# Earlier gathers for the expert mixer: aligned row places, the first two heads picked singly, five gathers ahead of the last two weight splits

## What is computed

```
q = (xt @ w_query).reshape(t, PEER_HEADS, 2, PEER_KEY_DIM // 2)          # 8 heads, 2 x 64
s = jnp.einsum('thkd,hknd->thkn', q, sub_keys)                           # 2 x 128 sub-keys a head
vals, idx = lax.top_k(s, PEER_TOPK)                                      # 16 of each
cand = (vals[:, :, 0, :, None] + vals[:, :, 1, None, :]).reshape(...)    # 256 sums
best, pos = lax.top_k(cand, PEER_TOPK)                                   # 16 experts a head
...
expert = (i1 * N_SUB_KEYS + i2).reshape(t, PEER_HEADS * PEER_TOPK)       # 128 picks a token
gate = jax.nn.softmax(best, axis=-1)
a = jnp.einsum('cd,ced->ce', xb, u_tab[eb])
w = gb * jax.nn.gelu(a, approximate=False)
out = jnp.einsum('ce,ced->cd', w, v_tab[eb])
```

## Time and profile before

| | us |
|---|---|
| median of 3 runs | 4531.28 (4531.2 to 4533.3) |
| profiled execution, its own time | 4529.67 |
| its span | 4527.9 |
| PE busy | 4151.7 (92%) |
| DVE busy | 2505.7 (55%) |
| POOL busy | 1957.4 (43%) |
| ACT busy | 1320.4 (29%) |
| software DMA queue (the gathers) | 536.9 MB, 28.6% of the 16 engines' span |

### The profile page before, as it was taken

One profiled execution on the slowest core, in us unless ns is written; L12 is line 12 of the kernel. 1 busy time (PEld: TensorE's weight loads), 2 busy tenths in 40 slices (PEclk: granted clock), 3 DMA queues, 4 the chain that ended last, 5 costly groups with the idle time before them and its releaser, 6 DMA issues.

```text
span 4527.9 us, 49208 instructions
## 1 busy us (share of the span) xinstructions
PE 4151.7 (92%) x15840; PEld 2816.4 (62%) x15840; DVE 2505.7 (55%) x4408; ACT 1320.4 (29%) x2903; POOL 1957.4 (43%) x1612
## 2 busy tenths in 40 slices
PE   7999987787787787899999999999999999999998
PEld 4567753333333333388876676888888867767886
DVE  7967676766767675544235545543343264536442
ACT  2224222222222222332223332322232233333322
POOL 4333543333333333354454353444444544445443
PEclk8999999989999999899999999999999999999999
DMA  5112279999999999732322121223223212112232
GB/s 140 42 59 82 79 317 421 421 421 421 421 412 421 421 406 422 292 102 95 96 84 65 44 91 63 94 97 94 95 96 96 95 56 70 59 63 95 96 94 83
DMA packets 160595, 806.06 MB, mean 178 GB/s; under 512 B 17488, under 2 KB 25088, under 8 KB 94848
## 3 DMA queue, kind: packets, MB, share of 16 engines
q0 software_dynamic: 73728, 536.90, 28.6%
q1 hardware_dynamic: 81952, 260.15, 17.8%
q10 hardware_dynamic: 4704, 6.42, 0.8%
HBM read 798.17 MB, written 5.24 MB: 177 GB/s over the span
## 4 chain that ended last, share of the span: by engine, by line
issue 27%; PE 25%; POOL 19%; DMA 14%; DVE 11%; DVEq 1%; ACT 1%; POOLq 1%; ACTq 0%
POOL wl L621 10%; PE bank L1015 6%; DMA rows_o<-in_peer_uv,expert 6%; POOL wl L590 6%; PE bank L674 5%; PE bank L676 5%; PE bank L675 5%; DMA rows_x<-in_peer_uv,expert 4%; DMA rows_w<-in_peer_uv,expert 4%; POOL wh L588 2%; DVE rows_o L2091 1%; DVE rows_w L2091 1%; DVE hst L1869 1%; DVE rows_x L2091 1%; POOLq L589 1%
## 5 line engine op out<-in xcount | busy, mean ns | idle before, releaser
L621 POOL TENSOR_TENSOR wl<-raw,wh 128x1024 fp32r<-128x1024 f32 (+3 forms) x304 | 726.4, 2390 | 831.1 <-ACT wh L1510 831.1
L674 PE MATMUL bank<-xh,wh 128*128 128x512 f32 x2368 | 945.0, 399 | 1.6 <-DVE oraw L2256 1.6
L676 PE MATMUL bank<-xh,wl 128*128 128x512 f32 x2368 | 924.9, 391 | 0.0
L675 PE MATMUL bank<-xl,wh 128*128 128x512 f32 x2368 | 923.3, 390 | 0.0
L674 PEld LDWEIGHTS bank<-xh,wh 128*128 128x128 f32 x2368 | 445.5, 188 | 144.0 <-issue 51.3
L1510 ACT ACTIVATE wh<-raw 128x1024 fp32r<-128x1024 f32 x304 | 320.7, 1056 | 729.5 <-PE bank L676 584.3
L676 PEld LDWEIGHTS bank<-xh,wl 128*128 128x128 f32 x2368 | 445.2, 188 | 95.0
L675 PEld LDWEIGHTS bank<-xl,wh 128*128 128x128 f32 x2368 | 446.0, 188 | 89.1 <-issue 1.9
L590 POOL TENSOR_TENSOR wl<-raw,wh 128x1024 fp32r<-128x1024 f32 (+2 forms) x234 | 479.2, 2048 | 34.8 <-issue 1.9
L1015 PE MATMUL bank<-rows_o,diag 128*128 128x512 f32 x688 | 340.8, 653 | 90.3 <-ACT diag L1476 90.3
L1015 PE MATMUL bank<-rows_w,diag 128*128 128x512 f32 x672 | 329.0, 647 | 95.0 <-ACT diag L1476 95.0
(11 more groups left out here) (414 smaller groups left out, 6432.0 us busy)
## 6 DMA issues: line engine op xcount, KB each, us to landing
raw<-in_w_l SPq DMA_DIRECT2D x324, 512.0 KB, 3.2
raw<-in_w SPq DMA_DIRECT2D x58, 512.0 KB, 3.2
raw<-in_w_l SPq DMA_DIRECT2D x64, 448.0 KB, 3.3
raw<-in_w_l SPq DMA_DIRECT2D x48, 256.0 KB, 2.6
raw<-in_w SPq DMA_DIRECT2D x16, 256.0 KB, 2.6
bias_scratch<-brow ACTq DMA_DIRECT2D x1, 3072.0 KB, 33.5
raw<-in_uq_l SPq DMA_DIRECT2D x16, 192.0 KB, 2.3
rows_o<-in_peer_uv,expert POOLq DMA_INDIRECT x172, 18.1
```

Source lines behind the costliest of these rows:

```text
L621: gp.tensor_tensor(wl[:, slot, 0:w], raw[:, rslot, 0:w], f32(wh[:, slot, 0:w]), ALU.subtract).then_inc(w_split.sem, 1)
L674: pe.matmul(bank[b][:], wh[:, slot, c], ah, start=k == 0, stop=False)
L675: pe.matmul(bank[b][:], wh[:, slot, c], al, start=False, stop=False)
L676: mm = pe.matmul(bank[b][:], wl[:, slot, c], ah, start=False, stop=k == last)
```

## The change

Five things, in one edit:

- The first buffer, the area behind the constants and `rows_o` start on multiples of 512 bytes, so that every row place does. `work` moves to behind `wl`, three small buffers become one.
- Heads 0 and 1 are picked one after the other instead of together. `SUB_KEY_PARTS` has (0, 0, 1), (0, 1, 1) in place of (0, 0, 2); PE forms the scores of head 0 after half of query 1 and those of head 1 after half of query 2. `p_pick` and `p_best` count one more.
- Gathers 0 to 4 stand ahead of POOL's splits of query 6 and 7. In these two splits the low part waits for the high part by a semaphore, `high_written`, in place of the drain.
- There are 14 row places for the first round and 13 from then on: `work` is one more, and `raw` serves once, for gather 5. The order is `o0` to `o3`, `work`, (`raw`), `w1`, `w3`, `w0`, `w2`, `x0` to `x3`. `w1` and `w3` wait for query 5 to be done, `w0` and all behind it for query 7.
- SP's first load of the second block waits until row 5, the one in `raw`, has been mixed.

`pick_experts` also copies the positions in two instructions, where it was one, in every window.

```diff
-        base = (nc.sbuf_base + 63) // 64 * 64
+        base = (nc.sbuf_base + 511) // 512 * 512
...
-        region = (top[0] + 127) // 128 * 128
+        region = (top[0] + 511) // 512 * 512
...
+        a.o = (a.o + 511) // 512 * 512
         rows_o = a("rows_o", [P, 4, 2 * D])
...
+        RING_ROWS = ["o0", "o1", "o2", "o3", "work", "w1", "w3", "w0", "w2", "x0", "x1", "x2", "x3"]
+        FIRST_ROWS = RING_ROWS[:5] + ["raw"] + RING_ROWS[5:]
+        row_of = FIRST_ROWS + [RING_ROWS[n % len(RING_ROWS)] for n in range(NB * PICKS - len(FIRST_ROWS))]
...
+        RAW_FREE = 1 + row_of.index("raw")
...
-        SUB_KEY_PARTS = [(0, 0, 2), (0, 2, 2), (0, 4, 4)] + [(tc, h0, 4) for tc in range(1, NB) for h0 in (0, 4)]
+        SUB_KEY_PARTS = [(0, 0, 1), (0, 1, 1), (0, 2, 2), (0, 4, 4)] + [(tc, h0, 4) for tc in range(1, NB) for h0 in (0, 4)]
...
+            sp.wait_ge(p_mixed, RAW_FREE)
...
-                gp.tensor_copy(wh[:, slot, 0:w], raw[:, rslot, 0:w])
-                gp.drain()
+                high = gp.tensor_copy(wh[:, slot, 0:w], raw[:, rslot, 0:w])
+                if behind_fetch:
+
+                    high.then_inc(high_written, 1)
+                    gp.wait_ge(high_written, behind_fetch)
+                else:
+                    gp.drain()
...
+            def fetch(n):
+
+                if n == 0 or n == TOPK:
+                    gp.wait_ge(p_pick, n // TOPK + 1)
+                elif n % WINDOW == 0:
+                    gp.wait_ge(p_pick, n // WINDOW + 2)
+                if row_of[n] == "raw":
+
+                    gp.wait_ge(w_split.sem, w_split.at(TILES_1, None))
+                if row_last[n] is not None:
+                    gp.wait_ge(p_mixed, row_last[n] + 1)
+                elif row_of[n] in ("w1", "w3"):
+
+                    gp.wait_ge(product.sem, product.at(TILES_1 - 2, None))
+                elif row_of[n] == "w0":
+
+                    gp.wait_ge(product.sem, product.at(TILES_1, None))
...
+            for j in range(6):
+                split(AT_1["query"].tile0 + j, None, KD)
+
+            for n in range(5):
+                fetch(n)
+            for j in range(6, 8):
+                split(AT_1["query"].tile0 + j, None, KD, behind_fetch=j - 5)
+            for n in range(5, NB * PICKS):
+                fetch(n)
...
-            linear(query, 1, None, normed)
+            linear(query, 1, None, normed, share=(0, 2))
+            pe.wait_ge(*read_at(query, 0, None))
+            sub_key_scores(0)
+            linear(query, 1, None, normed, share=(1, 2))
             linear(query, 2, None, normed, share=(0, 2))
-            pe.wait_ge(*read_at(query, 0, None))
             pe.wait_ge(*read_at(query, 1, None))
-            sub_key_scores(0)
+            sub_key_scores(1)
...
-            for q in range(2):
-                pick_keys(q)
-                pick_pairs(q)
-                pick_experts(q)
+            for q, heads in ((0, (0,)), (0, (1,)), (1, both)):
+                pick_keys(q, heads)
+                pick_pairs(q, heads)
+                pick_experts(q, heads)
```

More of the change, by code:

```diff
@@ L43 @@
 RAWS = 2
-ROWS = 12
 WINDOW = 2 * TOPK
@@ L305, in build @@
         rows_w = at("rows_w", [P, 4, 2 * D], F32, base + 4 * KD * T * 3 + 4 * RAWS * KD * P)
-        rows = [t[:, b, :] for t in (rows_o, rows_x, rows_w) for b in range(4)]
-        ROWS_W_FREE = 1 + max(n for n in range(NB * PICKS) if n % ROWS >= 8)
+        flat_row = lambda t: t[:].rearrange("p a t -> p (a t)")
+        row_tiles = {**{f"{c}{b}": t[:, b, :] for c, t in (("o", rows_o), ("x", rows_x), ("w", rows_w)) for b in range(4)},
+                     "work": flat_row(work), "raw": flat_row(raw)}
+        RING_ROWS = ["o0", "o1", "o2", "o3", "work", "w1", "w3", "w0", "w2", "x0", "x1", "x2", "x3"]
+        FIRST_ROWS = RING_ROWS[:5] + ["raw"] + RING_ROWS[5:]
+        row_of = FIRST_ROWS + [RING_ROWS[n % len(RING_ROWS)] for n in range(NB * PICKS - len(FIRST_ROWS))]
+        row_use = [row_of[:n + 1].count(r) for n, r in enumerate(row_of)]
+        row_last = [max([m for m in range(n) if row_of[m] == r], default=None) for n, r in enumerate(row_of)]
+        RAW_FREE = 1 + row_of.index("raw")
+        ROWS_W_FREE = 1 + max(n for n, r in enumerate(row_of) if r[0] == "w" and r != "work")
         psum = ctx.enter_context(nc.psum_tensor("bank", [P, 8 * T], F32))
@@ L379, in build @@
         p_gate = sem("p_gate")
-        fetched = [sem(f"fetched{i}") for i in range(ROWS)]
+        high_written = sem("high_written")
+        fetched = {r: sem(f"fetched_{r}") for r in FIRST_ROWS}
         p_dot = sem("p_dot")
@@ L571, in _, with split @@
             gp.wait_ge(made, 3)
-            def split(n, l, nblk, extra=0, turns=0):
+            def split(n, l, nblk, extra=0, turns=0, behind_fetch=0):
                 glob = n if l is None else TILES_1 + n
@@ L2008, in top16, with pick_keys @@
                 settle()
-            def pick_keys(q):
-                n = q if q < 2 else q // 2 + 1
+            both = (0, 1)
+            def pick_keys(q, heads=both):
+                n = heads[0] if q == 0 else 2 if q == 1 else q // 2 + 2
                 if q < 2 or q % 2 == 0:
-                    tc, h0, heads = SUB_KEY_PARTS[n]
+                    tc, h0, n_heads = SUB_KEY_PARTS[n]
                     h0 %= 4
@@ L2031, in pick_pairs, with pick_experts @@
                 settle()
[L2032 removed]
+                top16([(cand[:, h, :, :].rearrange("p a b -> p (a b)"), h) for h in heads], 2 * SUBK,
                       lambda key, o: best[:, key, o:o + 8], lambda key, o: pos[:, key, o:o + 8])
[L2035 to L2040 removed]
+            def pick_experts(q, heads=both):
+                hs = slice(heads[0], heads[-1] + 1)
+                grid = [P, len(heads), TOPK, TOPK]
+                dve.tensor_scalar(posh[:, 0, hs, :], pos[:, hs], 4, None, ALU.logical_shift_right)
+                dve.tensor_scalar(posh[:, 1, hs, :], pos[:, hs], 15, None, ALU.bitwise_and)
@@ L2051, in pick_experts @@
-                e0, e1 = (eid[:, k, :, :].rearrange("p h k -> p (h k)") for k in range(2))
+                cols = slice(q * WINDOW + heads[0] * TOPK, q * WINDOW + (heads[-1] + 1) * TOPK)
+                e0, e1 = (eid[:, k, hs, :].rearrange("p h k -> p (h k)") for k in range(2))
                 dve.scalar_tensor_tensor(expert[:, cols], e0, float(SUBK), e1, ALU.mult, ALU.add).then_inc(p_pick, 1)
-                dve.tensor_tensor(pgate[:, cols].rearrange("p (h k) -> p h k", h=2), best[:],
-                                  best[:, :, 0:1].to_broadcast([P, 2, TOPK]), ALU.subtract).then_inc(p_best, 1)
+                dve.tensor_tensor(pgate[:, cols].rearrange("p (h k) -> p h k", h=len(heads)), best[:, hs],
+                                  best[:, hs, 0:1].to_broadcast([P, len(heads), TOPK]), ALU.subtract).then_inc(p_best, 1)
```

73 lines of the change are left out of this document (32 added, 41 removed).

## The result

| | before | changed |
|---|---|---|
| median, us | 4531.9 (4531.2 to 4533.3, 4 runs) | 4488.4 (4487.8 to 4489.2, 4 runs) |
| profiled execution, its own time | 4529.67 | 4488.83 |
| its span | 4527.9 | 4486.7 |
| last dot product | 1889.62 | 1868.32 |
| from there to the end | 2638.3 | 2618.4 |

The ratio is 0.9904, 95% interval 0.9892 to 0.9916. The last two lines of the table show where to look: 21.3 us are gained by the last dot product, and 19.9 behind it, in the two layers that the forecast let "move as a whole".

A forecast was written before the change was run, and what follows sets the result against it. The gather stage's full DMA queue was taken as the bound, 2.48 us a gather. Terms 9.9 - 0.3 - 2.5 = 7.1 us off 4529.67 gave 4522.6, plus 1.6 for the median 4524.2; range 4517 to 4533.

The forecast's parts named there:

- move as a whole: Behind the last gather: the same dots, drain and splits follow unchanged, so no gain or loss there.
- Aligned places: Gather stage: row places on multiples of 512 bytes change nothing, priced at 0.
- The rival at 4500: Gather stage: alignment shortens packets, 24 us if half the fixed packet cost came from misaligned places; chance 8%.
- Eight gathers ahead, 9.9 us: Start of gather stage: eight instead of four gathers through before the wait for query 7 ends, 9.9 us gained.
- The lead: Gather 14, waiting for row 0 to be mixed: queue stays fed, gap 0 to 0.8 us, taken as 0.
- head 1's pass: DVE's picking of head 1 after head 0: 10.7 us, 60% of the two-head pass.
- SP's loads, 2.5 us: Second block's first two loads wait for row 5, about 631, into a full queue: 2.5 us lost.
- PE's scores, 0.3: PE before query 7's end: scores in three pieces instead of two add 0 to 0.65 us, taken as 0.3.
- the 13th place, 0: Block turns in blocks 3 and 4, where POOL pauses: the extra row place gains 0.
- POOL's arithmetic: Rival: splits of query 6 and 7 wait for the gathers issued ahead even without a drain; 4533.4 us, chance 7%.
- The semaphore: POOL's splits of query 6 and 7: waiting for its own instruction costs 0 to 0.5 us each, hidden.
- The holes at the block turns: Rival: DMA engines running dry at block turns costs time, the extra place saves about 4.9 us; 4519.3, chance 6%.

The follow-up runs named there:

- all_64: Kernel before, with first buffer, area behind the constants and rows_o all 64 bytes past a multiple of 256; 4512.2 us.
- all_128: Kernel before, with area behind the constants and rows_o 128 bytes past a multiple of 512, where first buffer and weights already lay; 4510.2 us.
- drained kernels: Changed kernel with the drain back in all splits in place of the semaphore, run twice; 4489.0 and 4490.4 us.

## Why the prediction was wrong, point by point

**Aligned places, priced at 0: this is the step that failed.** I had the right question and closed it with the wrong row. That 1 KB packets 128 bytes off took no longer than those on a multiple is true and stayed true: 46 ns at both in the packets of either trace. It says nothing about 8 KB packets in a queue that never empties; there the price was 4.4 ns on 309 in the mean and 0.033 us a gather, 16.9 us in all. The rival at 4500 had the sign and the place, at 24 us where the stage gave 17 to 18, but not the mechanism. A fixed cost of each packet would not spare the first three misaligned gathers in a row. The Trainium skill (DMA: Bandwidth & Descriptors, section How a descriptor splits into AXI transactions) would have come nearest for the gathers: 20 us by its extra beats, an estimate, for 16.9 measured. I said that the trace did not agree, from packets of another size. Its rule prices the unused bytes of each descriptor, and so explains neither the free gathers here nor that all_64, with half as many unused bytes, paid as much as all_128 (2.484 and 2.486 us a gather).

**No term for PE: the second step that failed.** The area with `hh` and the weights were both in the diff, moved from 128 bytes apart (within 256) to 0, and I read these lines as places for rows and `bias1` alone. I let the layers move "as a whole"; 17 to 20 us came from the distance. In the trace of before the clue stood in one view: matmuls of one shape at 391 ns on `xh` and 395 on `hh`, and I did not ask why.

**Eight gathers ahead, 9.9 us: right.** Gather 0 went out at 579.53 (forecast 579.6), gather 8 at 606.66 (606.7), and gather 7 had landed by 605.4 (604). Gather 13 landed at 625.2 (625.8) where before it landed at 634.2: 9.0 us gained at this point.

**The lead was not kept.** I took a gap of 0 (at most 0.8) at gather 14. Gather 14 landed 6.5 us after gather 13, a gap of 4.1, and the lead over before fell to 4.9 us. The failed term is head 1's pass: 10.7 us forecast, 15.8 measured, for a pass that stood beside two splits. The earlier trace rows held a pass beside splits too, but there the splits met mostly searches, which kept their time. 1.2 us of the gap are left without it, so 0 to 0.8 was also too little.

**SP's loads, 2.5 us: right.** The changed kernel has them at 636.34 (forecast 631), and the lead was 2.3 by gather 20; taking them away gave 2.8 to 2.9 in the stage.

**PE's scores, 0.3; the 13th place, 0: right within what can be read.** Query 7 ended at 606.4, where it had at 606.1.

Sum of the order's terms: 9.0 - 4.1 - 2.5 = 2.4, for the 7.1 of the forecast and the 2.2 to 3.3 of the profiles. (The upper end of the forecast's own range was summed 0.3 too low: its terms give 4527.7, not 4527.4. It changes nothing here.)

**Rivals.** POOL's arithmetic did not wait for the gathers: the cast ran at 585.72, right behind gather 4. The drain would have waited, though the split went on 0.7 us behind the last landing in both drained kernels and not 4.9. The semaphore cost 0.1 us (586.76 to 586.85), of the 0 to 0.5 that I allowed. The holes at the block turns gave nothing that could be told apart.

## What to carry to other kernels

Look for one shape of matmul at two mean durations in one profile, and compare the addresses of the moving operand and of the weights within 256 bytes; here a matching offset was worth 5 to 7 ns a matmul and some 18 us in all. Give row places of a full gather queue multiples of 256 bytes. And before pricing a moved instruction as hidden, ask which instructions it will now run beside: here two splits, in good time for PE, made DVE late by 5 us, and a wait of POOL's that only kept them off DVE's pass gained 2.

## What the runs showed of the hardware

- A float matmul of 128x512 on `hh` and `hl` took 389 ns where the addresses of its moving operand and its weights, taken within 512 bytes, differed by 0 or 256, 388 to 394 at 64, and 395 at 32 and 128. Moved weights slowed those on `xh` and `xl` in the same way, from 390 or 391 ns to 395.
- A gather of 128 rows of 8 KB into places off a multiple of 256 took 2.486 us, on it 2.453, at 64 off as at 128. The first three misaligned gathers behind aligned ones paid nothing, nor did four between eight aligned ones.
- POOL's subtraction (2.4 us) held up copies and two-operand instructions of DVE until it ended (2.39 and 2.46 us where 0.25 and 0.43 were usual), its cast (1.05 us) a shift and a comparison (0.54 and 1.10 for 0.17 and 0.42); DVE's searches beside them kept their 0.28 us.
- A drain on POOL waited 9.83 and 10.03 us for the five gathers issued ahead of it, and ended 0.7 us behind the last landing; an arithmetic instruction started as soon as the fifth was issued.
